# Level loop of a linear-attention mixer: gate tiles moved, fillers in quarters, exponentials reordered, queries compacted

## The chip, the core and the metric

The kernel runs on one core of a Trainium2 chip. The core has five engines that work side by side and wait for each other on semaphores: TensorE (PE; its weight loads are shown as PEld), VectorE (DVE), ScalarE (ACT), GpSimd (POOL) and SyncE (SP), which here only starts transfers from memory. The metric is the device time of one execution in microseconds (us); less is better.

## The reference, cut to what matters

The model has four layers on 512 tokens of width 1024, each a mixer and a feed-forward block. Layers one and two are of a first kind, which the change doesn't touch. Layers three and four (here "mixer 2", run twice) have three branches: two gated linear attentions (`hg` with 4 heads of key width 128, `gla` with 4 heads of key width 64) and a sparse attention (`nsa`). The change concerns the two linear attentions:

```
log_f = logaddexp(log(lb), log1p(-lb) + log_sigmoid(hf))
o_hg  = gated_linear_attention(silu(hq), -expm1(log_f), hi, log_f)
y_hg  = head_rmsnorm(o_hg) * silu(hog)
log_a = log_sigmoid(glr @ gla_w2 + gla_b) / 16
o_gla = gated_linear_attention(gq / 8, gk, gv, log_a)
y_gla = head_rmsnorm(o_gla) * silu(gog)
# attention: score(t, s) = sum_d q[t,d] * exp(b[t,d] - b[s,d]) * k[s,d] for s <= t,
# with b the running sum of the log decay; out = score @ v
```

## The kernel before

All activations lie transposed, 128 features on the partitions by 512 tokens. A dense product takes a weight tile (128 x 1024 float32) from a ring of three slots, which SyncE fills in the order of the stream. Each tile is split in two fp32r parts: high (`w_hi`, a rounded copy) and low (`w_lo`, the tile less its high part), two buffers of each. A tile is then 24 matmuls of 512 columns: `w_hi*h_hi`, `w_hi*h_lo`, `w_lo*h_hi` for eight blocks of the input. Normally GpSimd makes both parts (`times_one` at L1226, the subtraction at L1233).

**Ahead of the loop**, mixer 2 projects the keys `YKEYS[:BEFORE]` with `BEFORE = 21`: `hi`, `gv`, `nv`, `low`, `hf`, `gdec`, `hq`. ScalarE copies each product out of its bank (`copy_out`, L1491).

**The level loop** computes the decayed scores without dividing by a decay. For level v = 1 to 9, blocks of m = 2^(v-1) tokens are paired, queries in the second half of a pair meet keys in its first half. `lf` holds the prefix sums of the log decay and `X` the suffix sums. Per level ScalarE makes the query's exponential `Eq` from `lf` (L1581), then the key's `Ek` from `X` (L1586); VectorE adds to `X` (L1699), multiplies the query (L1696, into `qsl`, whose first halves stay zero), adds to `lf` (L1699), multiplies the key into `ksl` (L1696), and places the level before in the score matrix (`place`, L2035: for v below 8 a predicated copy of 512 columns from the bank, L2055, with a memset ahead). TensorE computes the scores: for v below 8 four products of 128 x 128 per head. `X` and `lf` depend on themselves from level to level. The loop runs over six groups `u` in `LIN`: four with one `hg` head, two with two `gla` heads of 64 rows each, and ten levels in each group (v = 0 needs no decay). In group u the head or heads of group u-1 are finished: TensorE multiplies by the values (`lin_pv`, "PV" in the text), ScalarE squares (`out_copy`), VectorE applies gain and gate (`lin_out`), TensorE sums over columns (`lin_sum`), ScalarE copies the sums (`out_sum`).

**Fillers.** The 20 remaining projections (`hog`, `gk`, `gq`, `gog`, `nq`, `nkc`, `nks`, `nkw`, `nvc`) are cut into halves of 12 matmuls, which TensorE computes between levels:

```
levels = (0, 1, 3, 5, 7, 9) if u < 4 else range(1, 9)
first = BEFORE + (3 * u if u < 4 else 12 + 4 * (u - 4))
FILL |= {(u, v): (YKEYS[first + n // 2], n % 2) for n, v in enumerate(levels)}
```

When a filler is done, ScalarE copies it out (L1528) and casts the high part of the tile two further on (`high`, L1534, 1024 columns); GpSimd then subtracts for the low part (L1233). Each engine runs its queue in order, so the place of these operations in ScalarE's queue, between the two exponentials of a level and the next level's, counts. Silu of the two output gates runs in the loop, on 2048 columns at once (L1597), in groups 1 and 4.

After the loop come the rotation of keys and queries, the compression products (62 and 1 moving columns), the sparse attention, the merge of the branches and the output product.

## Time and profile before

| | |
|---|---|
| median of 3 runs | 3600.61 us (3599.3 to 3605.64) |
| the profiled execution | 3593.86 us, its span 3592.1 us |
| TensorE busy | 93% of the span |
| VectorE, ScalarE, GpSimd busy | 41%, 21%, 52% |
| mean granted TensorE clock | 0.949 of full speed |

All rows come from the profiled execution. Times of rows are counted from the start of its span. A matmul record lasts longer than the matmul occupies the array, since matmuls overlap: what one costs is the distance from its start to the next one's. A float32 product that isn't fp32r appears as two records. In a timeline the bracket gives how long the engine was idle before the row, and which instruction ended the wait. "issue" is a wait that the trace doesn't explain.

### The profile page before, as it was taken

Reading aid. Unit: us, or ns where it says so; the run is one execution under the profiler, and the core shown is the slowest. Engines: PE = TensorE matmul, PEld = TensorE weight load, DVE = VectorE, ACT = ScalarE, POOL = GpSimd, SP = SyncE. Lnnn points to the kernel's source line nnn. Section 1 sums busy time; section 2 is a strip of 40 time slices with the busy share of each in tenths; the row PEclk is TensorE's granted clock in tenths of the full one; section 3 lists DMA queues with packets and bytes.
Section 4 is the critical chain, followed back from the end, with each engine's and each line's share of the span. In section 5 each row is a group of like instructions: output and inputs, shape, how many; then the busy total and the mean of one; then the engine's idle time right before and its main releaser. Section 6 shows DMA issues by size and latency. Waiting matters only on the chain.

```text
span 3592.1 us, 43639 instructions
## 1 busy us (share of the span) xinstructions
PE 3352.9 (93%) x15368; PEld 2587.9 (72%) x15368; DVE 1469.8 (41%) x2480; ACT 743.8 (21%) x1490; POOL 1873.9 (52%) x860
## 2 busy tenths in 40 slices
PE   6899999999999987888999999998888799999998
PEld 5688888678888766664666888877666466688886
DVE  4554422454430356646113444034565521244411
ACT  3310002321000242217101100023331530120001
POOL 3267777347777731110445777775111015477774
PEclk9999999999999998868999999999898799999998
DMA  3122222112222211110122222222111002222221
GB/s 109 42 90 94 93 94 94 53 65 91 94 94 97 83 59 42 36 42 1 61 80 94 96 93 94 94 84 78 40 42 36 18 27 97 86 93 94 93 94 64
DMA packets 71437, 263.01 MB, mean 73 GB/s; under 512 B 7920, under 2 KB 7920, under 8 KB 71152
## 3 DMA queue, kind: packets, MB, share of 16 engines
q1 hardware_dynamic: 71280, 260.98, 21.8%
q8 instruction: 91, 1.49, 0.2%
q14 instruction: 66, 0.54, 0.0%
HBM read 258.85 MB, written 2.10 MB: 73 GB/s over the span
## 4 chain that ended last, share of the span: by engine, by line
PE 61%; issue 16%; POOL 14%; DVE 4%; ACT 4%; POOLq 0%; DMA 0%; DVEq 0%; ACTq 0%; SPq 0%
PE bank L555 60%; POOL w_hi L1226 8%; POOL w_lo L1233 6%; PE bank L1117 1%; ACT w_hi L1534 1%; ACT arena L1656 1%; DVE arena L1699 1%; DVE rope L1696 0%; DVE arena L2200 0%; DVE arena L1696 0%; ACT arena L1645 0%; DVE rope L2260 0%; PE bank L835 0%; ACT act_hi L1362 0%; DVE h_lo L1723 0%
## 5 line engine op out<-in xcount | busy, mean ns | idle before, releaser
L1226 POOL TENSOR_TENSOR w_hi<-ring,cst 128x1024 fp32r<-128x1024 f32 x402 | 765.7, 1905 | 1226.4 <-PE bank L555 912.0
L1233 POOL TENSOR_TENSOR w_lo<-ring,w_hi 128x1024 fp32r<-128x1024 f32 x430 | 1063.8, 2474 | 432.5 <-ACT w_hi L1534 401.6
L555 PE MATMUL bank<-h_hi,w_hi 128*128 128x512 f32 x2256 | 920.7, 408 | 2.1 <-DVE h_lo L1723 2.1
L555 PE MATMUL bank<-h_lo,w_hi 128*128 128x512 f32 x2256 | 901.8, 400 | 0.0
L555 PE MATMUL bank<-h_hi,w_lo 128*128 128x512 f32 x2256 | 900.0, 399 | 0.0
L555 PEld LDWEIGHTS bank<-h_hi,w_hi 128*128 128x128 f32 x2256 | 430.3, 191 | 111.3 <-issue 4.6
L555 PEld LDWEIGHTS bank<-h_hi,w_lo 128*128 128x128 f32 x2256 | 431.1, 191 | 106.3
L555 PEld LDWEIGHTS bank<-h_lo,w_hi 128*128 128x128 f32 x2256 | 430.8, 191 | 101.6 <-issue 1.4
L555 PE MATMUL bank<-act_hi,w_hi 128*128 128x512 f32 (+1 forms) x1296 | 483.3, 403 | 18.2 <-DVE act_lo L1933 9.2
L555 PE MATMUL bank<-act_hi,w_lo 128*128 (+1 forms) x1056 | 421.6, 399 | 0.0
L555 PE MATMUL bank<-act_lo,w_hi 128*128 (+1 forms) x816 | 324.3, 397 | 0.0
L555 PEld LDWEIGHTS bank<-act_hi,w_hi 128*128 128x128 f32 x1296 | 249.1, 193 | 80.7 <-issue 13.5
L1696 DVE TENSOR_TENSOR sil<-sil,bank 128x512 f32<-128x512 f32 x176 | 120.8, 686 | 409.3 <-PE bank L555 402.4
L555 PE MATMUL bank<-arena 64*128 64x128 f32 (+17 forms) x1248 | 234.3, 442 | 50.2 <-DVE arena L2060 18.0
L1699 DVE TENSOR_TENSOR x<-x,bank 128x512 f32<-128x512 f32 x80 | 54.5, 684 | 491.5 <-PE bank L555 490.8
L555 PEld LDWEIGHTS bank<-arena 64*128 64x128 f32 (+4 forms) x1248 | 133.8, 201 | 145.7 <-issue 67.4
L555 PEld LDWEIGHTS bank<-act_hi,w_lo 128*128 128x128 f32 x1056 | 202.1, 191 | 45.9
L1761 DVE TENSOR_TENSOR act_lo<-sil,act_hi 128x512 f32 x88 | 230.3, 2618 | 10.5
L555 PE MATMUL bank<-arena,ring 128*128 128x512 f32 (+1 forms) x544 | 221.9, 552 | 7.2 <-DVE arena L2122 7.2
L1383 ACT ACTIVATE sil<-sil 128x512 f32<-128x512 f32 x88 | 55.6, 632 | 829.8 <-DVE sil L1696 829.7
L555 PEld LDWEIGHTS bank<-arena,ring 128*128 128x128 f32 x544 | 114.5, 223 | 109.0 <-issue 107.3
L555 PEld LDWEIGHTS bank<-act_lo,w_hi 128*128 128x128 f32 x816 | 155.0, 190 | 35.9
(232 smaller groups left out, 3113.6 us busy)
## 6 DMA issues: line engine op xcount, KB each, us to landing
ring<-wstream SPq DMA_DIRECT2D x480, 512.0 KB, 3.4
par<-params SPq DMA_DIRECT2D x5, 656.5 KB, 4.8
x<-xT SPq DMA_DIRECT2D x4, 512.0 KB, 6.6
outT<-h SPq DMA_DIRECT2D x4, 512.0 KB, 2.7
cst<-const SPq DMA_DIRECT2D x1, 1436.5 KB, 10.5
arena<-pos SPq DMA_DIRECT2D x1, 256.0 KB, 10.6
```

Source lines behind the costliest of these rows:

```text
L555: return pe.matmul(out, lhsT, rhs, start=start, stop=stop)
L1117: last = pe.transpose(bank[6 + e][:, (t - st) * P:(t - st + 1) * P], nprob[w % 2][e][:, off:off + P], C("ident"))
L1226: return po.tensor_tensor(out, a, C("ones")[:, 0:1].broadcast_to([P, n]), ALU.mult)
L1233: po.tensor_tensor(pair_[1], raw, pair_[0].bitcast(F32), ALU.subtract).then_inc(done.sem, 1)
L1383: sc.activation(sil[:, r, :], sil[:, r, :], ACT.Silu).then_inc(silu.sem, 1)
L1534: sc.activation(weights2(s)[0], ring[:, s % RING, :], ACT.Copy).then_inc(w2_a.sem, 1)
L1656: sc.activation(nprobT[e][:, PT0[st]:PT0[st] + (NT - st) * P], bank[6 + e][:, 0:(NT - st) * P], ACT.Copy).then_inc(ns_o.sem, 1)
L1696: return ve.tensor_tensor(out, a, b, ALU.mult)
L1699: return ve.tensor_tensor(out, a, b, ALU.add)
L1761: ve.tensor_tensor(lo, sil[:, r, :], hi.bitcast(F32), ALU.subtract).then_inc(act_ready.sem, 1)
```

## The change

Six edits, all in mixer 2:

1. `BEFORE` becomes 29. The eight output-gate tiles (`hog`, `gog`) are projected ahead of the loop, with Silu in their `copy_out`; GpSimd splits all 29 tiles ahead. `gog` moves forward in the stream. The in-loop Silus and their semaphore go.
2. The 12 fillers left are computed in quarters of 6 matmuls, eight quarters in each group.
3. `high` casts in two halves of 512 columns, behind the exponentials of a level, and waits until the filler that used the buffer is done. `copy_out` of a filler has a level of its own.
4. The low part of a filler's tile is made by VectorE, in two halves (`low`), with a new semaphore `w2_l` on which TensorE and SyncE wait; GpSimd has none of them left.
5. ScalarE makes the key exponential ahead of the query exponential; VectorE adds to `X` ahead of its wait for the query exponential.
6. The scaled queries are stored compactly (256 columns; `qsl` is half the size and needs no zeroes), so for levels 1 to 7 the products have 64 moving columns and the predicated copy 256 columns.

The diff, cut to its core:

```diff
         ksl = rope2
-        qsl = view(W0 + 4096, 2, T)
+        qsl = view(W0 + 4096, 2, T // 2)
...
+        BEFORE = 29
+        BY_SCALAR = BEFORE
+        OWN = ZS - BY_SCALAR
...
-                 ("gdec", 2, None), ("hq", 4, 15), ("hog", 4, 19), ("gk", 2, 23), ("gq", 2, 25), ("gog", 4, 27),
+                 ("gdec", 2, None), ("hq", 4, 15), ("hog", 4, 19), ("gog", 4, 23), ("gk", 2, 27), ("gq", 2, 29),
                  ("nq", 4, 31), ("nkc", 1, 35), ("nks", 1, 36), ("nkw", 1, 37), ("nvc", 1, 38)]
-        BEFORE = 21
...
-            levels = (0, 1, 3, 5, 7, 9) if u < 4 else range(1, 9)
-            first = BEFORE + (3 * u if u < 4 else 12 + 4 * (u - 4))
-            FILL |= {(u, v): (YKEYS[first + n // 2], n % 2) for n, v in enumerate(levels)}
+            levels = (0, 1, 3, 4, 5, 6, 7, 8) if u < 4 else (1, 2, 3, 4, 5, 6, 7, 8)
+            FILL |= {(u, v): (FILLERS[2 * u + n // 4], n % 4) for n, v in enumerate(levels)}
...
+            if BY_SCALAR <= s < ZS:
+                return w2_l(l, 2 * (s - BY_SCALAR) + 2)
+            return w2_split(l, s + 1 if s < ZS else s + 1 - OWN)
...
+                        for k in range(ND) if part is None else (2 * part, 2 * part + 1):
                             if name == "low":
...
                         if v < 8:
-                            parts = [(slice(t * P, t * P + P), slice(t * P, t * P + P), slice(t * P, t * P + P))
+                            n = P if v == 0 else P // 2
+                            parts = [(slice(t * n, t * n + n), slice(t * P, t * P + P), slice(t * n, t * n + n))
                                      for t in range(NT)]
+                        elif v == 8:
...
                                 lin_pv(l, head)
-                        if u >= 4 and v == 4:
+                        if u >= 4 and v == 8:
                             for head, _, _ in LIN[u - 1][4]:
                                 lin_sum(l, head)
                         if (u, v) in FILL:
                             project(*FILL[u, v])
                         if 0 < u < 4 and v == 2:
                             lin_pv(l, u - 1)
-                        if 0 < u < 4 and v == 6:
+                        if 0 < u < 4 and v == 7:
                             lin_sum(l, u - 1)
                 for head, _, _ in LIN[-1][4]:
...
-                    if BY_SCALAR <= s < ZS:
-                        halves(ring[:, t % RING, :], weights2(s), w2_a, l * w2_a.per + it * 6 + (s + 1 - BY_SCALAR),
-                               w2_split, True)
...
-                for s in range(21):
+                    n = s if s < BY_SCALAR else s - OWN
+                    halves(ring[:, t % RING, :], weights2(s), w2_h, l * w2_h.per + it * 6 + (w2_h.start + n + 1), w2_split)
...
+                for s in range(17):
...
-                        dst = {"hog": "hy", "gog": "gy", "gk": "gk", "nkc": "ck", "nks": "ks", "nkw": "kw", "nvc": "cv"}[name]
+                        dst = {"gk": "gk", "nkc": "ck", "nks": "ks", "nkw": "kw", "nvc": "cv"}[name]
                         last = sc.activation(m2[dst][:, i, :], b[:, :], ACT.Copy)
                     last.then_inc(y_out.sem, 1)
-                def high(s):
-                    sc.wait_ge(*tile_in(l, BASE2, PER2, s))
-                    sc.activation(weights2(s)[0], ring[:, s % RING, :], ACT.Copy).then_inc(w2_a.sem, 1)
+                def high(n, half):
+                    s = tile_of(FILLERS[n]) + 2
+                    if s >= ZS:
+                        return
+                    if half == 0:
+                        sc.wait_ge(*tile_in(l, BASE2, PER2, s))
+                        sc.wait_ge(*y_mm(l, BEFORE + n + 1))
+                    c = slice(half * TILE // 2, (half + 1) * TILE // 2)
+                    sc.activation(weights2(s)[0][:, c], ring[:, s % RING, c], ACT.Copy).then_inc(w2_a.sem, 1)
...
                 for u, q, k, lf, heads in LIN:
-                    for v in range(10):
+                    for v in range(1, 10):
                         m = (1 << v) >> 1
-                        if v >= 1:
-                            c9, c8 = 9 * u + v, 8 * u + v - 1
-                            if v == 1:
-                                sc.wait_ge(*(hf_l(l, u + 1) if u < 4 else gl_f(l, u - 3)))
-                            else:
-                                sc.wait_ge(*ln_p(l, c8))
-                            if c9 > 2:
-                                sc.wait_ge(*ln_q(l, c9 - 2))
-                            sc.activation(compact(m2["Eq"][c9 % 2], m), halves(lf, m, 1), ACT.Exp).then_inc(ln_e.sem, 1)
+                        c9, c8 = 9 * u + v, 8 * u + v - 1
                         if v >= 2:
                             sc.wait_ge(*ln_x(l, c8))
                             if c8 > 2:
                                 sc.wait_ge(*ln_k(l, c8 - 2))
                             sc.activation(compact(m2["Ek"][c8 % 2], m), halves(m2["X"], m, 0), ACT.Exp)\
                                 .then_inc(ln_f.sem, 1)
-                        if landed is not None:
-                            copy_out(landed)
-                            s = Y[landed][1] + landed[1] + 2
-                            if s < ZS:
-                                high(s)
-                        landed = FILL[u, v][0] if (u, v) in FILL and FILL[u, v][1] == 1 else None
-                        if (u, v) in ((1, 4), (4, 8)):
-                            gates = m2["hy" if u == 1 else "gy"].rearrange("p a b -> p (a b)")
-                            sc.wait_ge(*y_out(l, Y["hog" if u == 1 else "gog", 3][0] + 1))
-                            sc.activation(gates, gates, ACT.Silu).then_inc(og_s.sem, 1)
+                        if v == 1:
+                            sc.wait_ge(*(hf_l(l, u + 1) if u < 4 else gl_f(l, u - 3)))
+                        else:
+                            sc.wait_ge(*ln_p(l, c8))
+                        if c9 > 2:
+                            sc.wait_ge(*ln_q(l, c9 - 2))
+                        sc.activation(compact(m2["Eq"][c9 % 2], m), halves(lf, m, 1), ACT.Exp).then_inc(ln_e.sem, 1)
+                        if u > 0 and v in (1, 2):
+                            high(2 * u - 1, v - 1)
+                        if u > 0 and v == 3:
+                            copy_out(FILLERS[2 * u - 1])
                         if 0 < u < 4 and v == 4:
                             out_copy(u - 1)
-                        if 0 < u < 4 and v == 7:
-                            out_sum(u - 1)
-                        if u >= 4 and v == 2:
-                            for head, _, _ in LIN[u - 1][4]:
-                                out_copy(head)
-                        if u >= 4 and v == 5:
+                        if u >= 4 and v in (4, 5) and v - 4 < len(LIN[u - 1][4]):
+                            out_copy(LIN[u - 1][4][v - 4][0])
+                        if v in (6, 7):
+                            high(2 * u, v - 6)
+                        if v == 8:
+                            copy_out(FILLERS[2 * u])
+                        if u > 0 and v == 9:
                             for head, _, _ in LIN[u - 1][4]:
...
-                            at = CONST["ident"].start + v * P
+                        at = CONST["ident"].start + v * P
+                        if v == 0:
                             mask = cst[:, at:at + P].unsqueeze(1).broadcast_to([P, NT, P])
-                            src = b[:, :].rearrange("p (a b) -> p a b", a=NT)
-                            if v == 0:
-                                last = mul(diag4(hd % 2), src, mask)
-                            else:
-                                ve.memset(small[:, 60:61], 0.0)
-                                last = ve.copy_predicated(diag4(hd % 2), mask.bitcast(U32), src)
+                            last = mul(diag4(hd % 2), b[:, :].rearrange("p (a b) -> p a b", a=NT), mask)
+                        elif v < 8:
+                            m = 1 << (v - 1)
+                            n = P // (2 * m)
+                            mask = cst[:, at:at + P].rearrange("p (g two m) -> p g two m", two=2, m=m)[:, :, 1, :]
+                            ve.memset(small[:, 60:61], 0.0)
+                            last = ve.copy_predicated(
+                                diag4(hd % 2).rearrange("p a (g two m) -> p a g two m", two=2, m=m)[:, :, :, 1, :],
+                                mask.bitcast(U32).unsqueeze(1).broadcast_to([P, NT, n, m]),
+                                b[:, 0:T // 2].rearrange("p (a g m) -> p a g m", a=NT, m=m))
...
+                def low(n, half):
+                    s = tile_of(FILLERS[n]) + 2
+                    if s >= ZS:
+                        return
+                    ve.wait_ge(*w2_a(l, 2 * (s - BY_SCALAR) + half + 1))
+                    hi_, lo_ = weights2(s)
+                    c = slice(half * TILE // 2, (half + 1) * TILE // 2)
+                    ve.tensor_tensor(lo_[:, c], ring[:, s % RING, c], hi_[:, c].bitcast(F32), ALU.subtract)\
+                        .then_inc(w2_l.sem, 1)
                 group0 = 0
                 for u, q, k, lf, heads in LIN:
                     X = m2["X"]
-                    if u == 0:
-                        ve.memset(qsl[:, :, :], 0.0)
                     ve.memset(X, 0.0).then_inc(ln_x0.sem, 1)
...
                         qo, ko = qsl[:, c9 % 2, :], ksl[:, c9 % 2, :]
-                        ve.wait_ge(*ln_e(l, c9))
...
                         else:
                             ve.wait_ge(*ln_f(l, c8))
                         if 1 < v <= 8:
                             ve.wait_ge(*ln_p(l, c8))
                         if v <= 8:
                             add(halves(X, m, 0), halves(X, m, 0), ends(lf, m, 1)).then_inc(ln_x.sem, 1)
-                        mul(halves(qo, m, 1), halves(q, m, 1), compact(m2["Eq"][c9 % 2], m)).then_inc(ln_q.sem, 1)
+                        ve.wait_ge(*ln_e(l, c9))
+                        if v == 1:
+                            ve.wait_ge(*(y_out(l, Y["gq", u - 4][0] + 1) if u >= 4 else y_out(l, Y["hq", u][0] + 1)))
+                        mul(compact(qo, m), halves(q, m, 1), compact(m2["Eq"][c9 % 2], m)).then_inc(ln_q.sem, 1)
                         if v <= 8:
                             ve.wait_ge(*ln_x(l, c8 + 1))
                             add(halves(lf, m, 1), halves(lf, m, 1), ends(lf, m, 0)).then_inc(ln_p.sem, 1)
...
-                        if 0 < u < 4 and v == 5:
-                            lin_out(u - 1)
-                        if u >= 4 and v == 3:
-                            for hd, _, _ in LIN[u - 1][4]:
-                                lin_out(hd)
+                        if u > 0 and v in (3, 4):
+                            low(2 * u - 1, v - 3)
+                        if v in (8, 9):
+                            low(2 * u, v - 8)
+                        if u > 0 and v in (6, 7) and v - 6 < len(LIN[u - 1][4]):
+                            lin_out(LIN[u - 1][4][v - 6][0])
```

## Rows read from the trace of the kernel before

**Rows 1.** Page: busy time by engine; shares of the chain that ended last.
```profile
PE 3352.9 (93%) x15368; PEld 2587.9 (72%) x15368; DVE 1469.8 (41%) x2480; ACT 743.8 (21%) x1490; POOL 1873.9 (52%) x860
...
PE 61%; issue 16%; POOL 14%; DVE 4%; ACT 4%; POOLq 0%; DMA 0%; DVEq 0%; ACTq 0%; SPq 0%
```

**Rows 2.** Windows: stretch, busy us by engine, granted clock, DMA share, GB/s.
```profile
1366.00:1406.00 40.00, 32.64 (x164) 27.39 (x162) 24.11 (x53) 11.19 (x27) 7.21 (x3) 0.87 0.12 40
1495.40:1549.40 54.00, 46.76 (x274) 34.96 (x270) 31.64 (x72) 12.08 (x28) 7.18 (x3) 0.87 0.10 30
...
2483.20:2745.00 261.80, 211.72 (x1153) 169.41 (x1151) 158.71 (x352) 78.78 (x160) 47.61 (x20) 0.90 0.13 41
1283.70:1549.40 265.70, 215.75 (x1153) 172.96 (x1151) 158.67 (x352) 78.83 (x160) 47.49 (x20) 0.89 0.12 40
...
1561.00:1597.00 36.00, 36.00 (x138) 30.49 (x138) 13.20 (x21) 2.25 (x5) 8.78 (x4) 0.50 0.19 63
```

**Rows 3.** Level loop, layer one: waits, then VectorE's costliest group by line.
```profile
PE bank L555 <- DVE rope L1696: 36.0, 14, 4.5
...
L1699 DVE TENSOR_TENSOR rope<-rope,arena 128x256 f32<-128x256 f32 x48 | 52.2, 1087 | 76.7 <-ACT arena L1581 32.8 <-ACT rope L1581 24.7 <-ACT arena L1586 15.8
```

**Rows 4.** Timeline of one stall (start, us, engine): ScalarE, GpSimd, VectorE, TensorE.
```profile
1333.21 0.60 ACT L1528 ACTIVATE arena<-bank 128x512 f32<-128x512 f32 x1 [2.90 <-PE bank L555]
1333.70 1.05 ACT L1534 ACTIVATE w_hi<-ring 128x1024 fp32r<-128x1024 f32 x1
...
1334.83 2.39 POOL L1233 TENSOR_TENSOR w_lo<-ring,w_hi 128x1024 fp32r<-128x1024 f32 x1 [6.34 <-ACT w_hi L1534]
...
1335.45 2.05 DVE L1699 TENSOR_TENSOR rope<-rope,arena 128x256 f32<-128x256 f32 x1 [2.62 <-ACT rope L1581]
...
1338.56 2.08 PE L555 MATMUL bank<-arena,rope 128*128 128x128 f32 x8 [2.34 <-DVE rope L1696]
```

**Rows 5.** Timeline: VectorE through one level; then line 1761's durations, whole run.
```profile
1337.76 0.41 DVE L1699 TENSOR_TENSOR arena<-arena 128x256 f32<-128x256 f32 x1
...
1338.43 0.72 DVE L2055 COPY_PREDICATED arena<-cst,bank 128x512 f32<-128x512 uint32 x1
...
1339.09 0.43 DVE L1699 TENSOR_TENSOR rope<-rope,arena 128x256 f32<-128x256 f32 x1
...
1339.77 0.42 DVE L1699 TENSOR_TENSOR arena<-arena 128x256 f32<-128x256 f32 x1
...
L1761 DVE TENSOR_TENSOR act_lo<-sil,act_hi x88: 693/2706/2795, 249.5 to 3440.4; 128x512 f32 x84, 128x512 fp32r<-128x512 f32 x4
```

**Rows 6.** Timeline, TensorE, one head: filler half, scores, column sum, PV.
```profile
1333.90 2.32 PE L555 MATMUL bank<-arena 128*128 128x512 f32 x8
...
1347.30 0.48 PE L555 MATMUL bank<-h_hi,w_hi 128*128 128x512 f32 x1
...
1350.19 1.05 PE L555 MATMUL bank<-arena,rope 128*128 128x128 f32 x8
1351.08 0.95 PE L555 MATMUL bank<-cst,arena 128*128 128x1 f32 x8
```

**Rows 7.** Timeline, TensorE, two heads: PV after its wait, then scores.
```profile
1451.44 5.01 PE L555 MATMUL bank<-arena 128*128 128x512 f32 x24 [4.58 <-DVE arena L2060]
...
1459.37 1.16 PE L555 MATMUL bank<-arena,rope 64*128 64x128 f32 x16
...
1463.46 1.16 PE L555 MATMUL bank<-arena,rope 64*128 64x128 f32 x16
```

**Rows 8.** Timeline around the loop's start: ScalarE's last copy ahead of it, GpSimd's splits.
```profile
1283.89 0.60 ACT L1521 ACTIVATE arena<-bank 128x512 f32<-128x512 f32 x1 [5.00 <-PE bank L555]
...
1278.33 1.89 POOL L1226 TENSOR_TENSOR w_hi<-ring,cst 128x1024 fp32r<-128x1024 f32 x1 [0.87 <-PE bank L555]
1280.30 2.42 POOL L1233 TENSOR_TENSOR w_lo<-ring,w_hi 128x1024 fp32r<-128x1024 f32 x1
1283.93 1.89 POOL L1226 TENSOR_TENSOR w_hi<-ring,cst 128x1024 fp32r<-128x1024 f32 x1 [1.21 <-PE bank L555]
```

## What the change will do to the time

> **What bounds the kernel now.** I read the page first: TensorE is busy for 93% of the span, and the chain that ended last runs over TensorE for 61%, "issue" for 16% and GpSimd for 14% [rows 1]. So most of the time is bound by TensorE, and a change pays where TensorE is not full. The stretches show where that is. The level loop of mixer 2 runs from 1283.7 to 1549.4 us in its first layer (265.7 us) and from 2483.2 to 2745.0 in its second (261.8 us), with TensorE busy for 215.7 and 211.7 us and a granted clock of 0.89 and 0.90 [rows 2]. Some 50 us per layer are idle, and the busy part is inflated by half-clock pieces. A one-head group takes 40.0 us and the last, two-head one 54.0 [rows 2].
>
> Next I read who waits. VectorE's in-place additions to the suffix X (L1699, `rope<-rope,arena`) take 1087 ns on average and VectorE sits idle 76.7 us before them, for ScalarE's exponentials; TensorE's scores wait 36.0 us in the first layer for VectorE's scaled operand [rows 3]. One stall shows the cause. GpSimd subtracts the low part of a filler weight tile from 1334.83 to 1337.22, VectorE's addition starts at 1335.45 and ends at 1337.50, 2.05 us where 0.43 is usual, and TensorE's next scores start only at 1338.56 after 2.34 us idle [rows 4]. VectorE is stuck while GpSimd works on SBUF. Ahead of it ScalarE spent 0.60 us on copying the filler out and 1.05 on casting the next tile, before VectorE's exponentials [rows 4].
> The Trainium skill (SBUF — State Buffer, Who interferes with whom) says the pair of ports that VectorE and GpSimd share is an exclusive lock, held for a whole instruction; the stall agrees with it.
>
> **The sum before.** I price TensorE's pieces at full clock, start to start.
> Half a filler tile is 12 matmuls, 1347.30 to 1350.19 less 0.03, so 2.86 us; a quarter is 1.43. A level's scores are 8 records, 0.89 us, and the eight records of a column sum with one moving column take about the same; PV of a head is 2.2 us, its 2.32 less what the last record overlaps [rows 6]. For two heads of 64 rows a level of scores with half a filler is 4.09 us (1459.37 to 1463.46), so its scores cost 1.25 [rows 7]. Levels 8 and 9 have fewer products, some 1.3 us together for one head and 1.9 for two, an estimate from the same rate. Scores of a group: 8 x 0.9 + 1.3 = 8.5 us for one head, 8 x 1.28 + 1.9 = 12.1 for two.
>
> **The parts of the change.**
> (1) Eight tiles (hog, gog) leave the loop. Ahead of it a tile costs 5.60 us, and TensorE is full there: ScalarE waits 5.00 us for TensorE between its copies, while GpSimd needs 1.89 + 2.42 us per tile, and is idle the rest [rows 8]. 8 x 5.6 = 44.8 us, no gain in itself, but no loss: in the loop they cost as much. Silu is now part of their copies, beside other Silu copies; the two 2048-wide Silus of the loop go, with the table loads around them.
>
> (2) Fillers: 12 tiles remain, two per group, in quarters. TensorE per level is then score plus quarter, 0.9 + 1.43 = 2.33 us (two heads 2.7), evenly, where now a level has either nothing (and TensorE starves) or 2.86.
>
> (3) VectorE makes low parts in halves of 512. A 512-wide subtraction took 693 ns when undisturbed and 2706 in the median beside GpSimd [rows 5]; I take 0.61 start to start (0.69 less the overlap that its neighbours show), 4 per group, 2.4 us. GpSimd has no work in the loop after its first 4.3 us, so the stalls of 2 us, up to 18 per layer, one for each filler tile cast by ScalarE, go. ScalarE's cast is split as well, and is placed behind the exponentials; it waits for a finished filler, but a score that VectorE needs anyway is queued behind that filler, so nobody else waits longer.
>
> (4) Key exponential first. Undisturbed, a level takes 2.01 us of VectorE now (1337.76 to 1339.77), of which the predicated copy is 0.66 [rows 5]. The new order lets X be added while ScalarE works on the query's exponential, so the chain (addition 0.42, exponential 0.42, two hand-overs of 0.1 to 0.2, product 0.34) is 1.4 us and VectorE's own work decides: 4 x 0.335 + copy.
>
> (5) Compact queries. The copy reads 256 columns instead of 512, 0.66 - 0.27 = 0.39 us by the 256-wide against the 512-wide rows. VectorE: 1.73 us per level. For TensorE I take no gain from 64 moving columns: 128 columns and 1 column take the same 0.89 us per 8 records [rows 6]; the ends are 0 and half of the 0.9, 7 levels x 0.45 x 6 groups = 19 us per layer. I take the first, as the 1-column row lies on the other side of 64.
> The Trainium skill (TensorE: Matmul & The Clock Gate, LDWEIGHTS) has a weight load take its column count over 1.2 GHz, an estimate of 107 ns per record for 128, whatever moves. By it compacting gives TensorE nothing; the two rows agree.
>
> **Does VectorE or TensorE decide?** One-head group, VectorE: 9 levels of products and additions 11, full copy 0.65, seven compact 2.7, levels 8 and 9 1.25, lows 2.4, gate 0.65, memset 0.4: 19.1 us. TensorE: 8.5 + 8 x 1.43 + PV 2.2 + sum 0.9 = 23.1 us. Two heads: VectorE about 24.5, TensorE 12.1 + 11.4 + 2.4 + 1.0 = 26.9, and 30.1 in the last group, which has two PVs and two sums. TensorE decides everywhere, by 10 to 20%.
>
> After, per layer: first group 8.5 + 11.4 = 19.9; three of 23.1; 26.9; 30.1: 146.2 us. Added: 3.5 at the start, where GpSimd still splits the tile whose twin now starts at 1283.93 [rows 8]; 0.7 where PV waits for the last placement (4.58 us now [rows 7]); 1.2 at the end; 3 for one fall of the clock around the two sums of the last group; 1 us of unforeseen waits per group, 6. That is 160.6, with the moved tiles 205.4. First layer 265.7 - 205.4 = 60, second 261.8 - 205.4 = 56: 117 us. The profiled execution took 3593.9 us, the median of the runs is 3600.6. 3593.9 - 117 = 3477, times 3600.6/3593.9: about **3483 us**.
>
> **The rivals.**
> *VectorE sets the pace.* Its margin is small, and its 24.5 against 26.9 in the two-head groups leaves out every hand-over. If each of 54 levels waits 0.5 us on it, that is 27 per layer beyond my sum: 3483 + 48 = about 3530. For it: with two heads each level has two copies, and each carries a memset and waits for the copy ahead. Against it: before, levels with half a filler and no GpSimd op beside them run without a wait [rows 7]. Chance 0.20, 3505 to 3545.
>
> *Compact scores do shorten TensorE.* 19 us per layer at most, capped by VectorE's time: 3440 to 3455. Chance 0.10.
>
> *The clock falls (slower).* Compact scores leave the array idle for part of each record. The stage behind the loop, dense matmuls of 62 and 1 columns, runs at a granted clock of 0.50, 1.2 GHz, for all of its 36 us [rows 2]. If the loop's mix did the same, its 146.2 us would double: 205 + 146 = 351 against 265.7, 3600 + 2 x 86 = 3770. It decides once 60/146 = 41% of the loop's matmul time is at 1.2 GHz. Against it: 1.43 of each 2.33 us is 512-wide, and falls now follow idle pieces. Chance 0.04.
>
> *The change doesn't do what it says:* the waits have another origin (ring transfers, copies in order), the even fillers only shift them, and the moved tiles' time is all that changes hands. That is 3590 to 3605. The stall of [rows 4] with its GpSimd row beside it speaks against it. Chance 0.03.
>
> **How the numbers follow.** Forecast 0.63 (3455 to 3505). Range: 3440 takes in half the bound of part (5), 3535 most of the VectorE case. Faster by over 0.2% (7 us, about what a measurement of this kernel can tell from no change) 0.94, within 0.02, slower 0.04.
>
> **What the new profile would show.** The loop about 161 us long in both layers, its groups some 23, 27 and 31 us, granted clock above 0.95. L1699 additions at 0.42 us. No GpSimd row between the first 5 us of the loop and its end. Score records still 0.11 us apart with 64 columns. The gap of 4.58 us ahead of PV under 1 us. Copies ahead of the loop still 5.60 us apart. It is wrong if TensorE's idle time in the loop stays above 20 us per layer, if tiles ahead of the loop take longer than 5.6 us, or if the clock is below 0.85 in the loop.

## The result, and the profile after

The changed kernel takes 3460.31 us (median of 4 runs, 3458.69 to 3473.82) against 3599.95 of the kernel before (4 runs, 3595.35 to 3605.64): a ratio of 0.9621 over all runs, 95% interval 0.9599 to 0.9642 (the two medians alone give 0.9612), so 140 us less. The forecast was 3483, with 3440 to 3535 as its range. The profiled executions, 3593.86 and 3461.91 us, are 132 us apart.

The page after: busy time by engine, and the chain that ended last. TensorE's share rose from 93% to 96% with the same 15368 instructions [rows 1].

```profile
PE 3310.2 (96%) x15368; PEld 2560.1 (74%) x15368; DVE 1407.5 (41%) x2518; ACT 725.0 (21%) x1482; POOL 1856.5 (54%) x856
...
PE 63%; POOL 15%; issue 14%; DVE 5%; ACT 2%; POOLq 0%; DVEq 0%; DMA 0%; SPq 0%; ACTq 0%
```

Windows after, with the columns of [rows 2]: the stretch from where the loop used to start to where it starts now, the loops of both layers, the second group (one head), the fifth (two heads), the last (two heads), and the stage behind the loop.

```profile
1283.70:1331.10 47.40, 47.40 (x205) 38.20 (x204) 0.00 (x0) 4.81 (x8) 36.17 (x17) 1.00 0.27 89
1331.10:1481.50 150.40, 145.11 (x961) 119.01 (x959) 125.88 (x371) 64.40 (x148) 4.25 (x2) 0.99 0.13 43
2460.70:2611.20 150.50, 145.16 (x962) 119.11 (x960) 125.89 (x372) 64.39 (x148) 4.26 (x2) 0.99 0.13 43
1355.10:1377.70 22.60, 22.60 (x137) 19.60 (x136) 19.58 (x58) 10.74 (x25) 0.00 (x0) 1.00 0.15 48
1423.10:1450.20 27.10, 26.24 (x211) 19.95 (x212) 23.98 (x75) 10.89 (x25) 0.00 (x0) 1.00 0.12 40
1450.20:1481.50 31.30, 29.33 (x226) 21.83 (x222) 24.05 (x74) 10.14 (x24) 0.00 (x0) 1.00 0.11 35
1493.00:1529.00 36.00, 35.81 (x138) 30.50 (x138) 13.21 (x20) 2.25 (x5) 8.80 (x4) 0.51 0.20 63
```

The loop lasts 150.5 us in both layers, where it took 265.7 and 261.8 [rows 2]. Its six groups take 23.98, 22.65, 22.65, 22.75, 27.04 and 31.38 us, from the starts of their first scores. The eight moved tiles take 44.8 us, and the loop of the first layer starts 47.4 later. So the first layer saves 265.7 - 150.5 - 47.4 = 67.8 and the second 261.8 - 150.5 - 44.8 = 66.5, together 134 us, where 117 were forecast. At the end of the second loop the changed kernel is 134 us ahead (2745.0 against 2611.2); the rest of the program gives 2 back. The stage behind the loop is unchanged, at its granted clock of 0.51.

What TensorE waits for in the first layer's loop after, with total, count and longest. It waited 36.0 us in 14 places for `rope` [rows 3]; now 1.5 us in 4.

```profile
PE bank L565 <- DVE arena L1702: 2.5, 1, 2.5
PE bank L565 <- DVE rope L1702: 1.5, 4, 0.6
PE bank L565 <- DVE arena L2069: 0.4, 1, 0.4
```

### The profile page after: what moved, and what is told of

It reads as the page before. It is cut to its first block, busy times and chain, and to the rows that moved or that the text cites. A ratio compares the mean times of both kernels' runs of the same rounds, so it can differ in the third digit from the quotient of the medians.

```text
span 3460.1 us, 43641 instructions
## 1 busy us (share of the span) xinstructions
PE 3310.2 (96%) x15368; PEld 2560.1 (74%) x15368; DVE 1407.5 (41%) x2518; ACT 725.0 (21%) x1482; POOL 1856.5 (54%) x856
## 4 chain that ended last, share of the span: by engine, by line
PE 63%; POOL 15%; issue 14%; DVE 5%; ACT 2%; POOLq 0%; DVEq 0%; DMA 0%; SPq 0%; ACTq 0%
PE bank L565 61%; POOL w_hi L1238 9%; POOL w_lo L1244 6%; PE bank L1129 1%; ACT arena L1662 1%; DVE arena L1705 1%; DVE arena L2221 1%; DVE rope L1702 0%; DVE arena L1702 0%; ACT arena L1651 0%; DVE arena L2061 0%; DVE rope L1705 0%; DVE rope L2281 0%; ACT act_hi L1368 0%; DVE h_lo L1729 0%
## 5 line engine op out<-in xcount | busy, mean ns | idle before, releaser
L1238 POOL TENSOR_TENSOR w_hi<-ring,cst 128x1024 fp32r<-128x1024 f32 x418 | 795.9, 1904 | 1512.2 <-PE bank L565 935.8
L1244 POOL TENSOR_TENSOR w_lo<-ring,w_hi 128x1024 fp32r<-128x1024 f32 x410 | 1016.1, 2478 | 32.2
L565 PE MATMUL bank<-h_hi,w_hi 128*128 128x512 f32 x2256 | 909.2, 403 | 2.1 <-DVE h_lo L1729 2.1
L565 PE MATMUL bank<-h_hi,w_lo 128*128 128x512 f32 x2256 | 889.3, 394 | 0.0
L565 PEld LDWEIGHTS bank<-h_hi,w_hi 128*128 128x128 f32 x2256 | 421.9, 187 | 108.5 <-issue 4.6
L1705 DVE TENSOR_TENSOR x<-x,bank 128x512 f32<-128x512 f32 x80 | 54.5, 684 | 495.8 <-PE bank L565 495.0
L565 PE MATMUL bank<-arena 64*128 64x128 f32 (+19 forms) x1248 | 227.2, 437 | 29.3 <-DVE small L2221 13.8
```

The lines of the kernel that those rows point to most:

```text
L565: return pe.matmul(out, lhsT, rhs, start=start, stop=stop)
L1238: return po.tensor_tensor(out, a, C("ones")[:, 0:1].broadcast_to([P, n]), ALU.mult)
L1244: po.tensor_tensor(pair_[1], raw, pair_[0].bitcast(F32), ALU.subtract).then_inc(done.sem, 1)
L1705: return ve.tensor_tensor(out, a, b, ALU.add)
```

## The experiments

Loop lengths and groups below are of the profiled execution: a group runs from the start of its first score to that of the next group, the last one to the start of the last heads' product with the values (PV). "Per layer" compares them with the 150.5 us after. Absolute medians should be compared within a set only: beside e1 to e4 the kernel before took 3600.23 us, beside e5 to e8 3595.68, beside e9 to e12 3591.47, and beside the changed kernel 3599.95. Between the sets, ratios and loop lengths count. e5 and e11 start from the kernel before, all others from the changed one.

**e5: the tiles moved, and nothing else.** Core of the edit to the kernel before:

```diff
+        BEFORE = 29
-            levels = (0, 1, 3, 5, 7, 9) if u < 4 else range(1, 9)
+            levels = (0, 3, 5, 7) if u < 4 else (2, 4, 6, 8) if u == 4 else (1, 3, 5, 7)
```

> The kernel before with one part alone: the eight output-gate tiles ahead of the loop (Silu in their copies), the remaining 12 fillers in halves, two tiles per group; GpSimd low parts, old order, wide queries. Theory: each filler tile in the old loop brought about 3.8 us of waits and slow clock (11.5 us over three tiles of a one-head group), so 8 tiles fewer save about 30 us per layer, less what the levels now bare of fillers add: 3535 to 3570 us. Rival (moving was nearly the whole gain): 3460 to 3480. Rival (moving gives nothing without the other parts): 3590 to 3605.

Measured: 3613.24 us, 1.0056 of before (1.0038 to 1.0074): a little slower, where I had expected 25 to 60 us less. The loop takes 223.1 and 224.7 us; with the 44.8 ahead of it 267.9 and 269.5, more than the 265.7 and 261.8 of before. Waits and window of its loop, and one stall, with the columns of [rows 4]:

```profile
PE bank L554 <- DVE rope L1688: 45.3, 16, 4.6
...
1327.40:1550.40 223.00, 171.84 (x961) 140.76 (x959) 142.14 (x352) 58.25 (x138) 27.88 (x12) 0.84 0.09 29
...
1342.34 0.60 ACT L1524 ACTIVATE arena<-bank 128x512 f32<-128x512 f32 x1 [4.55 <-PE bank L554]
1342.83 1.05 ACT L1530 ACTIVATE w_hi<-ring 128x1024 fp32r<-128x1024 f32 x1
1343.78 0.41 ACT L1577 ACTIVATE arena<-arena 128x256 f32<-128x256 f32 x1
...
1343.96 2.34 POOL L1232 TENSOR_TENSOR w_lo<-ring,w_hi 128x1024 fp32r<-128x1024 f32 x1 [11.96 <-ACT w_hi L1530]
...
1344.58 2.00 DVE L1691 TENSOR_TENSOR rope<-rope,arena 128x256 f32<-128x256 f32 x1 [4.38 <-ACT rope L1582]
...
1347.72 2.07 PE L554 MATMUL bank<-arena,rope 128*128 128x128 f32 x8 [4.61 <-DVE rope L1688]
```

With four halves in a group instead of six, TensorE waits longer (45.3 us for `rope` against 36.0), and the granted clock of the loop is 0.84 instead of 0.89. The stall shows the chain. ScalarE waits 4.55 us for the filler's end, copies it and casts the next tile, and only at 1343.78 makes the next level's exponentials; VectorE has idled 4.38 us. Then GpSimd's subtraction stretches VectorE's addition to 2.00 us, and TensorE has idled 4.61 us. The fillers had covered part of such chains; taken away they lay the chain bare. Moving the tiles alone costs time. It does so although e5 also takes the two in-loop Silus out of ScalarE's queue: in the kernel before, the one of group 1, with the two loads of function tables around it (1.28 us each), keeps a level's exponentials (1338.60) and the next level's (1344.02) 5.4 us apart.

**e11: e5 plus the later place of ScalarE's copies and casts.** Everything else stays as before: halves, query first, wide queries, low parts of 1024 columns by GpSimd. Edit to e5, in ScalarE's queue behind the exponentials of a level:

```diff
-        FILL[4, 1] = FILL.pop((3, 7))
...
-                        if landed is not None:
-                            copy_out(landed)
-                            s = Y[landed][1] + landed[1] + 2
+                        if (u > 0 and v == 1) or v == 6:
+                            n = 2 * u if v == 6 else 2 * u - 1
+                            s = Y[YKEYS[BEFORE + n]][1] + YKEYS[BEFORE + n][1] + 2
...
+                                sc.wait_ge(*y_mm(l, BEFORE + n + 1))
...
+                        if u > 0 and v == 3:
+                            copy_out(YKEYS[BEFORE + 2 * u - 1])
+                        if v == 8:
+                            copy_out(YKEYS[BEFORE + 2 * u])
```

> The kernel of e5 (before, with only the eight tiles moved) with one more part: copies and casts of the 12 fillers at the levels that the changed kernel uses (cast at 6 and 1, copy at 8 and 3), behind a filler that has long ended; halves, query exponential first, wide queries and GpSimd low parts of 1024 stay. Theory (the place of copies and casts is the main gain): groups of 26 instead of 36 us, the loop 165 to 185 instead of 227 us, 3490 to 3530 us. Rival (the gain needs quarters, order and compact queries together): 3580 to 3613.

Measured: 3507.46 us, 0.9765 (0.9737 to 0.9793), 106 us less than e5 and in the range expected; the loop takes 171.6 and 169.9 us. Its waits and its window:

```profile
PE bank L553 <- DVE rope L1691: 14.4, 15, 1.7
...
1335.30:1506.90 171.60, 151.82 (x961) 123.55 (x959) 141.69 (x352) 59.32 (x138) 28.73 (x12) 0.96 0.12 38
```

GpSimd still subtracts ten times per layer, and VectorE does nearly the same work, yet the longest wait for `rope` falls from 4.6 to 1.7 us. The place of the copies and casts in ScalarE's queue is worth 51.4 and 54.8 us per layer. In the first layer 31 of the 51 are waits of TensorE (51.2 against 19.8 us), and 20 are matmuls that last shorter at the higher clock (busy 171.8 against 151.8 us, 961 records both times). (One filler half also goes back from the first level of the fifth group to the fourth group; the first three groups, which it doesn't touch, shrink by 10 to 12 us each all the same.)

**e9: that place undone in the changed kernel.**

```diff
-                        if u > 0 and v in (1, 2):
-                            high(2 * u - 1, v - 1)
-                        if u > 0 and v == 3:
-                            copy_out(FILLERS[2 * u - 1])
...
+                        if (v == 5 and FILL.get((u, 4), (0, 0))[1] == 3) or v == 9:
+                            n = 2 * u + (v == 9)
+                            if n != 7:
+                                copy_out(FILLERS[n])
+                            for half in range(2):
+                                high(n, half)
```

> The changed kernel with one thing undone: ScalarE copies a filler out and casts both halves of the next tile at the level behind the filler's last quarter (levels 5 and 9), as the old loop did, ahead of the next level's exponentials; only the copy of one filler (nq 3) stays late, as its target is still read. Theory (what starved TensorE was ScalarE's wait for a filler just computed, with the exponentials queued behind it): filler end, copy 0.6, casts 1.1, exponentials 0.8, four VectorE operations 1.4 make 4 us, against 2.2 us that TensorE has in hand, so about 1.9 us for each of ten to twelve tiles per layer: 3495 to 3510 us. Rival (the halving and the reordered work of the levels matter, the place of the copies doesn't): 3460 to 3466.

Measured: 3493.39 us, 0.9726 (0.9703 to 0.975), just under the range expected, with a loop of 161.7 and 165.5 us, 11 and 15 more per layer. Every one-head group takes 24.9 us or more, where the change has 22.65 to 23.98.

**e10: e9, and the low parts back on GpSimd, 1024 columns at once.**

```diff
+                    po.tensor_tensor(lo_, ring[:, s % RING, :], hi_.bitcast(F32), ALU.subtract)\
+                        .then_inc(w2_l.sem, 2)
```

> The kernel of e9 (early copies and casts) with the low parts made by GpSimd in one piece of 1024, VectorE making none. Theory (the lock costs only where VectorE is late already): GpSimd's 2.4 us start behind the cast, beside the exponentials, and hold VectorE 1.5 us longer than e9 does, about 15 us per layer: 30 us above e9. Rival (no lock on the path, as in e1): equal to e9 or some us below it.

Measured: 3564.71 us, 0.9922 (0.9898 to 0.9945), 71 us above e9, where 30 were expected; the loop takes 203.8 and 201.8 us. One stall of it, and its window:

```profile
1369.02 2.42 POOL L1297 TENSOR_TENSOR w_lo<-ring,w_hi 128x1024 fp32r<-128x1024 f32 x1 [12.50 <-ACT w_hi L1551]
...
1369.32 2.40 DVE L1706 TENSOR_TENSOR arena<-arena,rope 128x256 f32<-128x256 f32 x1 [1.97 <-ACT rope L1602]
...
1371.85 1.10 PE L565 MATMUL bank<-arena 128*128 128x64 f32 x8 [1.57 <-DVE arena L1706]
...
1334.60:1538.50 203.90, 172.87 (x962) 137.29 (x960) 134.64 (x351) 62.69 (x148) 28.10 (x12) 0.85 0.10 32
```

The cast right ahead of the exponentials releases GpSimd at the moment when VectorE has come late by the same cast. Both delays add, TensorE runs dry, and the granted clock drops to 0.85, from 1.00 in e9. The clock is the larger part: of the 42.2 us that separate the first layer's loops, 15.2 are waits of TensorE (31.0 against 15.9 us) and 27.0 the same 962 records lasting longer (busy 172.87 against 145.84 us). e9's waits for `rope` are 1.4 us at the longest, e10's 3.4. Clock included, each of the ten subtractions per layer costs 3.6 us more than on VectorE.

**e1: the low parts back on GpSimd in the changed kernel, in halves of 512.**

```diff
+                        po.tensor_tensor(lo_[:, c], ring[:, s % RING, c], hi_[:, c].bitcast(F32), ALU.subtract)\
+                            .then_inc(w2_l.sem, 1)
...
-                            low(2 * u - 1, v - 3)
...
-                            low(2 * u, v - 8)
```

> The changed kernel with the low parts of the ten filler tiles in the loop made by GpSimd again, in halves. Theory (TensorE decides in the loop, VectorE has about 3 us to spare per one-head group): VectorE loses up to 1.2 us behind each half and saves 0.6, so most of it is hidden: 3460 to 3475 us. Rival (the shared access of GpSimd and VectorE was the main cost of the old loop, 2 us for each tile on the path): 10 tiles x 2 us x 2 layers = 40 us more, about 3500.

Measured: 3464.07 us, 0.9633 (0.9596 to 0.967); loop 150.2 and 150.1 us: no difference to the change that the runs can tell. One-head groups take 0.28 us more, the last one 1.45 less. VectorE is busy for 123.25 us of the loop against 125.88: it loses about as much to GpSimd's subtractions as its own took (a product beside one lasts 1.52 us instead of 0.42), and it has room for it. So part (3)'s change of engine gains nothing once the casts are late. e1 has halves and e10 whole tiles; with late casts the size is worth little, since e11 has whole tiles (an addition beside one lasts up to 2.31 us) and late casts, and stays 32 us (0.9765 less 0.9677, times 3600) above e2, of which e3 and e4 may explain 6 and 19. What halves on GpSimd would cost beside early casts wasn't run.

**e2, e3, e4: one part undone each.** Two quarters at one level in place of one at each of two; query exponential first; wide queries with the 512-column copy.

```diff
-            levels = (0, 1, 3, 4, 5, 6, 7, 8) if u < 4 else (1, 2, 3, 4, 5, 6, 7, 8)
+            levels = (0, 0, 3, 3, 5, 5, 7, 7) if u < 4 else (1, 1, 3, 3, 5, 5, 7, 7)
```

> The changed kernel with the same two filler tiles per group, but each in two halves of 12 matmuls (two quarters in one level: levels 0, 3, 5, 7 or 1, 3, 5, 7) instead of eight quarters. Theory (VectorE needs 1.73 us for a one-head level and works one level ahead while TensorE is in a half of 2.8 us): about 1 us of waits per group, 3465 to 3480 us. Rival (even filling is what removed the waits): each of four bare levels per group waits 0.9 to 1.5 us, 6 groups x 2 layers x 5 us = 60 more, about 3520.

```diff
                         sc.activation(compact(m2["Eq"][c9 % 2], m), halves(lf, m, 1), ACT.Exp).then_inc(ln_e.sem, 1)
+                        if v >= 2:
+                            sc.wait_ge(*ln_x(l, c8))
...
+                            sc.activation(compact(m2["Ek"][c8 % 2], m), halves(m2["X"], m, 0), ACT.Exp)\
```

> The changed kernel with the old order of exponentials: the query's first, and VectorE waits for it before it adds to X. Theory (TensorE decides): a level of VectorE goes from 1.73 to about 2.0 us, under TensorE's 2.25, so 3460 to 3466 us. Rival (the chain through the exponentials sets the pace): 0.3 to 0.5 us for each of 54 levels in 2 layers, 3490 to 3515.

```diff
-        qsl = view(W0 + 4096, 2, T // 2)
+        qsl = view(W0 + 4096, 2, T)
...
+                                last = ve.copy_predicated(diag4(hd % 2), mask.bitcast(U32), src)
```

> The changed kernel with the scaled queries stored wide again: 128 moving columns in the scores of levels 1 to 7, predicated copies of 512 columns. Theory (score records are bound by the weight load at either width, VectorE has room in one-head groups and little in two-head ones): scores of a level still 0.81 us, 1 to 2 us more in each two-head group, 3463 to 3472 us. Rival (compact queries shorten TensorE): 7 levels x 0.45 us x 6 groups x 2 = 38 more, about 3498.

| | us | ratio (95%) | loop | groups |
|---|---|---|---|---|
| e2 halves | 3477.52 | 0.9677 (0.9637 to 0.9718) | 156.6 / 156.7 | 25.2 23.2 23.2 23.3 29.7 31.9 |
| e3 query first | 3466.00 | 0.964 (0.9603 to 0.9677) | 151.2 / 151.3 | 24.3 22.65 22.65 22.75 27.2 31.6 |
| e4 wide queries | 3479.69 | 0.9674 (0.9633 to 0.9715) | 155.2 / 155.2 | 23.4 22.6 22.6 22.7 29.0 34.8 |

Quarters are worth 6.2 us per layer in the loop, and 1.6 right behind it, where e2's PV of the last two heads lasts 6.19 us instead of 4.58; the order of the exponentials is worth 0.8, which the medians can't tell from nothing, and compact queries 4.7. None of e4's one-head groups gets longer (the first is 0.6 us shorter, which stays unexplained); the gain lies in the two-head groups (2.0 and 3.4 us), where VectorE makes two copies per level. It was more than expected.

**e6: VectorE 0.6 us longer per level**, by a reduction that nobody reads.

```diff
+                        ve.reduce_max(spare[:, c9 % 8:c9 % 8 + 1], C("cos2"), AX_X)
```

> The changed kernel with one more VectorE instruction per level, a maximum over 512 columns into a spare column, about 0.6 us, which nobody waits for; nothing is left out. Theory (TensorE decides, VectorE has 3 us to spare in a one-head group): 5.4 us more work per group, 2.4 of them beyond the room, some 13 us per layer: 3475 to 3495 us. Rival (VectorE sets the pace already): 54 x 0.6 us per layer, about 3525. Rival (VectorE far from the bound): 3460.

Measured: 3502.44 us, 0.975 (0.9728 to 0.9773), 7 us above the range expected; groups of the first layer 25.2, 25.4, 24.9, 25.0, 31.9, 37.5. One-head groups lose 1.2 to 2.75 of the 5.4 us added (nine times 0.6 from start to start), so they had some 3 us of room. The two-head groups lose 4.8 and 6.1, about all of it, the last one at a granted clock of 0.91: they had none.

**e7: TensorE 1.4 us less per group**, three of 24 matmuls of each filler left out (the output is then not the reference's).

```diff
-                        for k in range(ND) if part is None else (2 * part, 2 * part + 1):
+                        for k in range(ND) if part is None else (2 * part, 2 * part + 1) if part < 3 else (7,):
```

> The changed kernel with 3 of the 24 matmuls of each filler tile left out (the block k = 6 of the last quarter), so its output is not the reference's. Theory (TensorE decides in the loop): 12 x 3 x 0.234 us = 8.4 us less per layer, about 3443 us. Rival (VectorE or the hand-overs decide): the time stays at 3460.

Measured: 3458.66 us, 0.9616 (0.9597 to 0.9636). The one-head groups take 22.67, 21.25, 21.25, 21.35: 1.40 less in each of the last three, which is six matmuls of 0.23. The two-head groups of the first layer take 27.02 and 35.68, no less and 4.3 more; those of the second layer 31.54 and 31.73, 4.5 and 0.35 more. Instead of the 17 us expected, next to nothing is gained. Two score levels of the fifth group, then three matmuls and the window of a stretch of the last:

```profile
1425.16 1.11 PE L565 MATMUL bank<-arena,rope 64*128 64x64 f32 x16 [0.58 <-DVE rope L1702]
...
1428.01 1.11 PE L565 MATMUL bank<-arena,rope 64*128 64x64 f32 x16 [0.86 <-DVE rope L1702]
...
1457.37 1.97 PE L565 MATMUL bank<-arena,rope 64*128 64x64 f32 x16 [0.84 <-DVE rope L1702]
1459.27 0.79 PE L565 MATMUL bank<-h_hi,w_hi 128*128 128x512 f32 x1
1459.86 0.63 PE L565 MATMUL bank<-h_lo,w_hi 128*128 128x512 f32 x1
...
1457.40:1466.90 9.50, 9.50 (x46) 7.19 (x46) 7.37 (x25) 2.60 (x7) 0.00 (x0) 0.50 0.14 52
```

TensorE decides in the one-head groups to the tenth of a microsecond. In the two-head groups the time taken from it turns into waits for VectorE. Behind two such waits the clock falls to 1.2 GHz for 9.5 us, in the last group of the first layer, which gives most of the rest back; in the second layer the fifth group has waits of 0.60 and 0.84 us, with matmuls of 0.63 us behind them and a granted clock of 0.84. The fifth group of the first layer has the same waits without a fall, which stays unexplained.

**e8 and e12: two versions that might beat the change.** Both give level 0 of the first group two quarters, where VectorE is held up anyway. e8 moves VectorE's low parts from levels 3 and 4 to 2 and 4; e12 gives those of the two-head groups to GpSimd. The edit of e8:

```diff
+            levels = (0, 0, 1, 3, 4, 5, 6, 7) if u == 0 else (0, 1, 3, 4, 5, 6, 7, 8) if u < 4 else (1, 2, 3, 4, 5, 6, 7, 8)
...
-                        if u > 0 and v in (3, 4):
+                        if u > 0 and v in (2, 4):
```

> The changed kernel with two small moves: in the first group two quarters at level 0 and none at level 8, to fill the wait of 2.9 us there, and VectorE's low parts of the odd fillers at levels 2 and 4 instead of 3 and 4, to spread them in the two-head groups (waits of 0.7 and 0.2 us before the scores of levels 4 and 5). Theory: 1.4 to 2.9 us and about 1.5 us less per layer, 3452 to 3457 us. Rival (the wait of the first group only moves behind the second quarter): 3460.

> The changed kernel with two quarters at level 0 of the first group (none at its level 8) and, in the two-head groups alone, the low parts by GpSimd, as the last group was 1.5 us shorter in e1 while the one-head groups were 0.3 us longer. Theory: loop 150.5 - 1.5 - 1.6 = about 147.5 us, 3453 to 3457 us. Rival (nothing that a measurement tells): 3460.

Measured: 3459.71 us, 0.9625 (0.9611 to 0.9639), and 3462.01 us, 0.9638 (0.9617 to 0.9659). The first group drops from 23.98 to 22.24 in both, but the second group takes 23.0, and the last group of one layer 1.3 to 1.6 us more than that of the other (granted clock 0.95 there), so that the loops last 149.0 to 150.5 us. e12's fifth group takes 28.4 us, 1.35 more than with VectorE's low parts. Both had been expected at 3452 to 3457 us; no version here measurably beats the changed kernel.

## Why the prediction was right, and where it was not

**Direction, place and mechanism.** The gain lies in the level loop of both layers, and TensorE is what is left as the bound in the one-head groups (e7). The stall of [rows 4] is gone; the additions of L1705 (then L1699) take 422 ns on average where they took 1087 [rows 3].

**The sum.** Forecast 160.6 us for the loop, measured 150.5. Its terms, in us:

| term | forecast | measured |
|---|---|---|
| first group with its start | 19.9 + 3.5 = 23.4 | 23.98 |
| three one-head groups | 3 x 23.1 = 69.3 | 68.05 |
| fifth group with PV's wait | 26.9 + 0.7 = 27.6 | 27.04 |
| last group, its end, the clock's fall | 30.1 + 1.2 + 3 = 34.3 | 31.38 |
| unforeseen waits | 6 | in the rows above |

The two terms that failed are paddings: 6 us of unforeseen waits, and 3 us for a fall of the clock around the last two sums, which doesn't come (granted clock 1.00 in that group). They are 9 of the 10 us per layer. The rest is mostly the price of a level's scores. I took 0.89 us, and 1.43 for a quarter; TensorE's rows in the second group show 0.81 from start to start, with 128 moving columns (level 0) and with 64 (level 1) alike, and 1.48 for the quarter behind them:

```profile
1355.07 1.05 PE L565 MATMUL bank<-arena 128*128 128x128 f32 x8
1355.88 0.48 PE L565 MATMUL bank<-h_hi,w_hi 128*128 128x512 f32 x1
...
1357.36 1.00 PE L565 MATMUL bank<-arena 128*128 128x64 f32 x8
1358.17 0.48 PE L565 MATMUL bank<-h_hi,w_hi 128*128 128x512 f32 x1
```

**Part (1), the moved tiles: price right, role wrong.** They cost 44.8 us ahead of the loop, at 5.60 each. "In the loop they cost as much" was wrong: without them, and without their Silus, the loop is 42.6 and 37.1 us shorter (e5), so in a loop bound by chains a tile cost 5.3 and 4.6 us, as it filled waits. Whether the move gains anything once the chains are short isn't shown: no run leaves the tiles in the loop with the other parts in place.

**Part (2), quarters: right.** 2.29 us per level (1357.36 to 1359.65) against 2.33; undone they cost 7.8 us per layer (e2).

**Part (3), the step that was argued wrongly.** I named the port that VectorE and GpSimd share as the cause of the stalls, and mentioned in a half-sentence that the cast is "placed behind the exponentials". The runs show the reverse order of weight. The late place alone brings 106 us over both layers with GpSimd still subtracting (e5 to e11). In the changed kernel the four combinations of place and engine take 3564.71 us (early, GpSimd; e10), 3493.39 (early, VectorE; e9), 3464.07 (late, GpSimd; e1) and 3460.31 (late, VectorE). (e10 subtracts a whole tile at once, e1 in halves.) The place is worth 100 to 104 us with GpSimd and 33 to 38 with VectorE, by medians and by ratios; the engine 71 us while the casts are early (36 to 42 per layer in the loop), and nothing that can be told once they are late. The two delays lie in one chain, and together they cost far more than one by one. The number didn't depend on which of the two I blamed, since the change removes both: that it came out is in this respect luck.

The Trainium skill (SBUF — State Buffer, Who interferes with whom) says that the one that comes second blocks until the first is through; the 2.40 us row of e10 agrees, while e1 shows that such a block costs nothing on an engine with room. Late in a level, the chain now reads on ScalarE: two exponentials as soon as their inputs are there, and the copy of a filler behind them.

```profile
1357.63 0.42 ACT L1589 ACTIVATE rope<-rope 128x256 f32<-128x256 f32 x1 [0.69 <-DVE rope L1705]
1358.37 0.42 ACT L1597 ACTIVATE rope<-arena 128x256 f32<-128x256 f32 x1 [0.33 <-DVE arena L1705]
1358.70 0.59 ACT L1534 ACTIVATE arena<-bank 128x512 f32<-128x512 f32 x1
```

**Part (4), key exponential first: harmless.** 0.8 us per layer (e3). The chain through ScalarE decides in neither order, once nothing stands in its way.

**Part (5), compact queries.** "No gain for TensorE" held for one head: 0.81 us at both widths, and e4's one-head groups no longer. With two heads a level's scores take 1.03 us against 1.09 (e4), some 0.4 us in a group. The Trainium skill (TensorE: Matmul & The Clock Gate, LDWEIGHTS) gives an estimate of 107 ns per weight load; with one head the rows have a record every 0.10 us, which agrees with it; with two heads of 64 rows they have one every 0.065 us (1.03 for sixteen), less than such a load, so the estimate isn't the bound there. The 56 copies of 256 columns last 522 ns on average; 0.39 us start to start was forecast, and the second group shows 0.53 (1360.69 to 1361.22) and 0.34 (1363.74 to 1364.08).

**"TensorE decides everywhere, by 10 to 20%": false in two of six groups.** The forecast for VectorE there, 24.5 us, left out the hand-overs, as its rival said. VectorE is busy 23.98 of 27.10 us in the fifth group, and TensorE is still made to wait before two of its levels:

```profile
1435.31 1.11 PE L565 MATMUL bank<-arena,rope 64*128 64x64 f32 x16 [0.61 <-DVE rope L1702]
...
1438.17 1.11 PE L565 MATMUL bank<-arena,rope 64*128 64x64 f32 x16 [0.15 <-DVE rope L1702]
```

e4, e6 and e7 show it from three sides. It cost no accuracy, which is luck: the two engines' sums lie so close there that TensorE's alone came out within 1.3 us. The rival "VectorE sets the pace" is thus true for the two-head groups, without its price of 0.5 us in each of 54 levels. (That rival's sum has a slip: twice 27 us are 54, not 48.)

**The start of the loop.** The forecast's 3.5 us is this stall: GpSimd splits the last tile made ahead, first high, then low, and VectorE's first product stands until it is through. Part of the wait isn't GpSimd's: ahead of the first exponential ScalarE loads a function table, 1.28 us from 1331.90, and the product starts only at 1333.75. Undisturbed, at 0.42 us, it would have ended 1.8 us earlier (an estimate), so some 0.7 of TensorE's 2.46 us would stay. Behind the wait the matmuls last 0.63 us instead of 0.40, up to 1341.68.

```profile
1331.33 1.89 POOL L1238 TENSOR_TENSOR w_hi<-ring,cst 128x1024 fp32r<-128x1024 f32 x1 [1.20 <-PE bank L565]
1333.31 2.36 POOL L1244 TENSOR_TENSOR w_lo<-ring,w_hi 128x1024 fp32r<-128x1024 f32 x1
...
1333.75 2.19 DVE L1702 TENSOR_TENSOR arena<-arena 128x256 f32<-128x256 f32 x1 [53.41 <-ACT arena L1597]
...
1336.00 1.10 PE L565 MATMUL bank<-arena 128*128 128x64 f32 x8 [2.46 <-DVE arena L1702]
...
1338.04 0.63 PE L565 MATMUL bank<-h_hi,w_hi 128*128 128x512 f32 x1
```

**The listed signs.** Groups of 23, 27 and 31 us, clock above 0.95, additions at 0.42, no GpSimd row between 1335.67 and the end of the loop, tiles ahead 5.60 apart: all seen. The wait of 4.58 us ahead of PV [rows 7] is 0.37:

```profile
1451.59 4.58 PE L565 MATMUL bank<-arena 128*128 128x512 f32 x16 [0.37 <-DVE arena L2069]
```

**The other rivals.** A low clock in the loop didn't come (0.99), nor did cheaper compact scores. "The change doesn't do what it says" was right in one point: the waits did have another main origin, copies in order, than the one I gave; but the change removes that one as well.

**What stays open.** Undone one by one, the parts cost 0.8, 4.7, 7.8, 0 and 11 to 15 us per layer, 24 to 28 together, while the change saves 67. The parts cover for each other, and behind e10's long waits comes a low clock, so no single undoing measures a part's share; e5 to e11 and e9 to e10 are the steps here that show a large one. The moved tiles were never put back alone. Which of cast and copy-out does the harm when placed early wasn't tried.

## What to carry to other kernels

When one operation of a fixed queue waits for another engine's result, ask what stands behind it in that queue: here copies and casts of filler work ahead of the next level's exponentials cost 51 to 55 us per layer, which moving them brought back. Filler work that covers waits is worth more inside a chain-bound loop than outside; so shorten the chain before you think of moving the work. For the sum of a loop, take the price of a piece from rows without a wait around it, and don't pad what every row explains.

## What the hardware showed that I had not expected

- Less work for TensorE can cost time: in e7 the last group of the first layer got 4.3 us longer with six matmuls fewer; behind waits of 0.60 and 0.84 us the clock ran at 1.2 GHz for 9.5 us. The fifth group of the second layer got 4.5 us longer.
- GpSimd's subtraction beside VectorE costs between nothing (e1) and 3.6 us apiece (e10), by what stands ahead of it in ScalarE's queue. Two thirds of the latter is matmuls at a lower clock, not waiting (27.0 of 42.2 us in the first layer).
- One record of a float32 product takes 0.10 us of TensorE at 1, 64 and 128 moving columns. With two heads of 64 rows, sixteen records take 1.03 us at 64 columns and 1.09 at 128 (e4), 0.065 and 0.068 each.
